# A two-layer hybrid decoder step in fp32: retention heads first, the gate chain spread over three quads, residual updates chunk by chunk

## What is computed

```python
h = rmsnorm(x, norm_mix_pre)
# one projection w_in, its columns shared out among 4 mLSTM, 4 retention and 8 gated-DeltaNet heads
proj = h @ w_in
y = concat(mlstm(...), retention(...), gated_delta(...)) @ w_out
x = x + rmsnorm(y, norm_mix_post)
h = rmsnorm(x, norm_mlp_pre)
x = x + rmsnorm(square(relu(h @ w_up)) @ w_down, norm_mlp_post)
```

## Time and profile before

| | us |
|---|---|
| median of 3 runs | 3286.99 (3285.19 to 3288.15) |
| the profiled execution | 3280.49 |
| its span | 3278.9 |
| TensorE busy in it | 3122.5 (95%) |
| DVE busy | 1930.1 (59%) |
| ACT busy | 1535.4 (47%) |

### The profile page before, as it was taken

The page is one execution under the profiler, slowest core; times in us unless marked ns, Lnnn a source line. Parts: engine busy times, 40 slices in busy tenths (PEclk is TensorE's granted clock), DMA queues, the critical chain, the costliest instruction groups (busy, mean ns, idle before and its releaser), DMA issues.

```text
span 3278.9 us, 72394 instructions
## 1 busy us (share of the span) xinstructions
PE 3122.5 (95%) x23264; PEld 3057.9 (93%) x23264; DVE 1930.1 (59%) x3923; ACT 1535.4 (47%) x3564; POOL 84.5 (3%) x161
## 2 busy tenths in 40 slices
PE   5999999998999999999869999999989999999997
PEld 5989999998999999999869989999989999999997
DVE  5677755656545545455567777556665455454555
ACT  4566654544433334334446666545444333343333
POOL 0000000000000000000010000000000000000000
PEclk9999999999999999999989999999999999999999
DMA  3344455643544444544423444555435444444454
GB/s 132 128 133 135 132 162 161 185 155 110 175 166 159 164 164 166 166 160 164 151 84 121 131 132 137 168 167 177 155 118 167 165 164 167 162 163 164 163 167 147
DMA packets 266061, 499.24 MB, mean 152 GB/s; under 512 B 34272, under 2 KB 39552, under 8 KB 265664
## 3 DMA queue, kind: packets, MB, share of 16 engines
q1 hardware_dynamic: 243360, 443.56, 41.3%
q0 software_dynamic: 14496, 51.05, 4.7%
q10 hardware_dynamic: 8064, 2.80, 0.3%
HBM read 475.30 MB, written 22.01 MB: 152 GB/s over the span
## 4 chain that ended last, share of the span: by engine, by line
PE 79%; DVE 9%; ACT 5%; issue 4%; DMA 2%; DVEq 1%; ACTq 0%; SPq 0%; POOLq 0%; POOL 0%
PE PU L455 71%; PE PABCD L455 4%; PE PE_ L455 2%; ACT Y L787 2%; PE PF L455 2%; ACT AE L787 1%; DVE WL L1156 1%; DMA RAW<-in_w 1%; ACT WH L787 1%; DVE Y L1170 1%; PE PABCD L458 1%; DVE Y L1321 1%; DVE AE L1500 1%; DVE X L1173 0%; PE PE_ L458 0%
## 5 line engine op out<-in xcount | busy, mean ns | idle before, releaser
L455 PE MATMUL PU<-HH,WH 128*128 128x288 f32 x4096 | 1285.4, 314 | 59.3 <-DVE HL L1161 48.0
L787 ACT ACTIVATE WH<-RAW 128x512 fp32r<-128x512 f32 x1669 | 965.2, 621 | 591.9 <-PE PU L455 437.5
L455 PE MATMUL PU<-HL,WH 128*128 128x288 f32 x4096 | 1212.6, 296 | 0.0
L455 PE MATMUL PU<-HH,WL 128*128 128x288 f32 x4096 | 1208.7, 295 | 0.0
L1156 DVE TENSOR_TENSOR WL<-RAW,WH 128x512 fp32r<-128x512 f32 x1668 | 1074.5, 687 | 223.0 <-ACT WH L787 205.8
L455 PEld LDWEIGHTS PU<-HH,WH 128*128 128x128 f32 x4096 | 774.6, 189 | 79.2 <-DVE HL L1161 49.4
L455 PEld LDWEIGHTS PU<-HL,WH 128*128 128x128 f32 x4096 | 775.8, 189 | 7.0
L455 PEld LDWEIGHTS PU<-HH,WL 128*128 128x128 f32 x4096 | 775.0, 189 | 0.0
L455 PE MATMUL PU<-UH,WH 128*128 128x288 f32 x2560 | 759.0, 296 | 3.2 <-DVE UL L1310 2.0
L455 PE MATMUL PU<-UL,WH 128*128 128x288 f32 x2560 | 755.2, 295 | 0.0
L455 PE MATMUL PU<-UH,WL 128*128 128x288 f32 x2560 | 752.7, 294 | 0.0
(11 more groups left out here) (245 smaller groups left out, 2244.4 us busy)
## 6 DMA issues: line engine op xcount, KB each, us to landing
RAW<-in_w SPq DMA_DIRECT2D x1669, 256.0 KB, 3.7
SIN<-in_sin POOLq DMA_DIRECT2D x32, 512.0 KB, 4.2
out_sout<-Y POOLq DMA_DIRECT2D x32, 512.0 KB, 5.3
BC<-gate_rows POOLq DMA_DIRECT2D x32, 304.0 KB, 4.3
AUX<-in_aux POOLq DMA_DIRECT2D x32, 152.0 KB, 3.4
X<-in_x SPq DMA_DIRECT2D x4, 576.0 KB, 7.5
out_y<-X SPq DMA_DIRECT2D x4, 576.0 KB, 2.8
Y<-in_gw POOLq DMA_DIRECT2D x2, 1024.0 KB, 5.0
```

Of the source, the lines that this page charges most:

```text
L455: return nc.tensor.matmul(out, lhsT, rhs, start=start, stop=stop, skip_group_check=True)
L787: return nc.scalar.activation(out, in_, f, **kw)
```

## The change

- **Order of heads.** After "first" come the four retention heads, then gated-DeltaNet (its first front stands in the last retention quad), then mLSTM. SP loads the units in that order from the same array; POOL's and ACT's stores go to the same places; `turn_of` gives the order of chunks in the output projection.
- **Gate projection.** GWf becomes two halves GW[0] (in SIN) and GW[1] (in Z1), loaded by `load_gate_weights` at the program's start, and for layer 1 behind the last head of layer 0; DVE multiplies them between the first splits of layer 0, and for layer 1 in the first `down_last` quad. TensorE makes the 16 matmuls in slots 0 to 7 of "first", two a slot, beside the norm's sums.
- **Gate chain.** Steps up to "decay" in "first" (slots 8 to 21), copies and scans in retention quad 0 (DVE: slots 1, 2, 3, 16, 28; ACT: 18, 20, 22), transposes and columns in retention quad 1 (slots 0, 2, 8). Several scratch tiles get other rooms. POOL's `store_rows` stands before the third retention head.
- **Chunk by chunk.** `update_and_split` follows each update of a pair with the HL of the pair before, and with a weight split after pairs 2, 4 and 6, both in `after_out` and at the turn to layer 1. ACT's `prenorm` makes HH and squares of each pair and the pieces 5 to 7 between. At the very start ACT and DVE go piece by piece through weights and x. The outer loop over layers is written out twice.

```diff
@@ walk
-            with eng.Fori(0, DEPTH) as l:
+            for l in range(DEPTH):
...
-                quad(q0, "first", l, None, (n0, l * H_C, 0, 0, p0))
+                quad(q0, "first", l, None)
+                for k in range(H_B - 1):
+                    quad(q0 + 1 + k, "ret", l, ret_head(k))
+                quad(q0 + H_B, "ret", l, ret_head(H_B - 1), gdn_head(0, 0, 0))
...
@@ POOL
+            def load_gate_weights(l):
+                if l:
+                    held("head_done", HEADS * l + 1)
+                    held("state_decayed", HEADS * l)
+                    held("state_read", HEADS * l)
+                for j in range(2):
+                    pool.dma_start(GW[j], d["gw"][l, :, j * (NC_ // 2):(j + 1) * (NC_ // 2)]).then_inc(sem("gate_weights_in"), 16)
...
             pool.dma_start(NG0[:], d["ng0"][0]).then_inc(sem("first_gain_in"), 16)
+            load_gate_weights(0)
             held("constants_in", 16 * len(con))
...
+                held(*gate("proj", l))
+                load_state(n0 + H_C)
+                for k in range(H_B):
+                    if k == 2:
+                        store_rows(l)
+                    head(n0 + k, n0 + H_C + k, n0 + H_C + k + 1 if k < H_B - 1 else n0, k % 2)
...
@@ TensorE
+            def gate_part(t, kind, l):
+                if kind == "first" and t < 8:
+                    if t == 0:
+                        pe.wait_ge(*gate("weights_a", l))
+                    if t == 4:
+                        pe.wait_ge(*gate("weights_b", l))
+                    if l == 0 and t % 2 == 0:
+                        pe.wait_ge(sem(f"x_in{t // 2}"), 16)
+                    pe.wait_ge(sem("x_updated"), 16 * l + t + 1)
+                    for k in (2 * t, 2 * t + 1):
+                        i = mm(PD[:, 0:T], GW[k // 8][:, k % 8], X[:, k], k == 0, k == NC_ - 1)
...
                 for t in range(SLOTS):
+                    if l:
+                        gate_part(t, kind, l)
+                    norm_part(t, kind, l, x)
                     unit_part(Q, t, kind, l, x, last_head is not None)
-                    norm_part(t, kind, l, x)
+                    if not l:
+                        gate_part(t, kind, l)
+                    if kind == "ret" and x[2] < 2:
+                        gates(t, x[2], l, x)
@@ ACT, prenorm
+                for g in range(NC_ // 2):
+                    if e == 0 and l == 0 and g % 2 == 0:
+                        hi_part(Q, g // 2)
+                        act.wait_ge(sem(f"x_in{g // 2}"), 16)
+                    act.wait_ge(sem("x_updated"), 16 * l + 4 * e + g + 1)
+                    for c in (2 * g, 2 * g + 1):
                         fn(HH[:, c], X[:, c], scale=gain[:, c:c + 1]).then_inc(sem("hh_ready"), 1)
+                    for c in (2 * g, 2 * g + 1):
+                        if c >= 4:
+                            act.wait_ge(sem("squares_summed"), NC_ * (2 * l + which) + c - 3)
                         fn(SQ[:, c % 4], X[:, c], ACT.Square).then_inc(sem("squares"), 1)
+                    if (e or l) and g in (1, 3, 5):
+                        hi_part(Q, g // 2 + 5)
+                if e == 0 and l == 0:
+                    for piece in range(4, 8):
+                        hi_part(Q, piece)
                 norm_scale("squares_summed", NC_ * (2 * l + e // 2 + 1), S, "s_ready")
...
@@ DVE
+            def update_and_split(l, which, gain, lo_l, lo_which, lo_gain, Q):
+                for g in range(8):
+                    update_x(l, which, gain, g)
+                    if g:
+                        prenorm_lo(lo_l, lo_which, lo_gain, range(2 * g - 2, 2 * g))
+                    if g in (2, 4, 6):
+                        lo_part(Q, g // 2 + 3)
+                prenorm_lo(lo_l, lo_which, lo_gain, range(14, 16))
+                lo_part(Q, 7)
+
+            def split_first(l):
+                if l:
+                    return
+                for c in range(4):
+                    lo_part(0, c)
+                    prenorm_lo(0, 0, NG0, range(4 * c, 4 * c + 4))
+                    if c < 2:
+                        gate_weights(0, c)
+                for piece in range(4, 8):
+                    lo_part(0, piece)
...
             def after_mlp(l):
-                for g in range(8):
-                    update_x(l, 1, NG[:, 2], g)
+                if l < DEPTH - 1:
+                    update_and_split(l, 1, NG[:, 2], l + 1, 0, NG0, (l + 1) * QUADS)
```

More of the change, by code:

```diff
@@ L260, in gdn_pair @@
                         h = 2 * i + par
-                        after = None if last and par else (n0 + h + 1, l * H_C + h + 1, h + 1, 1 - par, p0 + i + par)
-                        quad(q0 + 1 + h, "gdn", l, (n0 + h, l * H_C + h, h, par, p0 + i), after)
+                        after = None if last and par else gdn_head(h + 1, 1 - par, i + par)
+                        quad(q0 + 1 + H_B + h, "gdn", l, gdn_head(h, par, i), after)
                 with eng.Fori(0, H_C // 2 - 1) as i:
@@ L266, in walk @@
                 gdn_pair(H_C // 2 - 1, True)
-                with eng.Fori(0, H_B // 2) as i:
-                    for par in range(2):
-                        h = 2 * i + par
-                        quad(q0 + 1 + H_C + h, "ret", l, (n0 + H_C + h, l * H_B + h, h, par, p0 + H_C // 2 + i))
                 for h in range(H_A - 1):
@@ L341, in _, with next_units @@
                 sp.dma_start(X[:, k], d["x"][:, k]).then_inc(sem(f"x_in{c}"), 16)
-                load(c, 0)
+                load(c, 4 * H_C)
             for n in con:
                 sp.dma_start(con[n][:], d[n]).then_inc(sem("constants_in"), 16)
-            with sp.Fori(0, DEPTH * QUADS) as Q:
+            def next_units(Q, unit, after):
                 for s in range(4):
@@ L349, in _ @@
                         sp.wait_ge(sem("lo_ready"), 16 * Q + 4 * s + c + 1)
-                        load(c, 4 * Q + s + 1)
+                        load(c, unit + s + 1 if s < 3 else after)
+            for l in range(DEPTH):
+                q0, u0 = l * QUADS, l * (4 * QUADS)
+                with sp.Fori(0, H_B - 1) as k:
+                    next_units(q0 + k, u0 + 4 * H_C + 4 * k, u0 + 4 * H_C + 4 * k + 4)
+                next_units(q0 + H_B - 1, u0 + 4 * (H_C + H_B - 1), u0)
+                with sp.Fori(0, H_C - 1) as h:
+                    next_units(q0 + H_B + h, u0 + 4 * h, u0 + 4 * h + 4)
+                next_units(q0 + H_B + H_C - 1, u0 + 4 * (H_C - 1), u0 + 4 * (H_C + H_B))
+                with sp.Fori(H_C + H_B, QUADS - 1) as q:
+                    next_units(q0 + q, u0 + 4 * q, u0 + 4 * q + 4)
+                q = QUADS - 1
+                next_units(q0 + q, u0 + 4 * q, u0 + 4 * (QUADS + H_C) if l < DEPTH - 1 else 4 * DEPTH * QUADS)
             sp.wait_ge(sem("lo_ready"), 16 * DEPTH * QUADS + 1)
@@ L437, in _ @@
[L437 to L446 removed]
+                load_parameters(n0 + H_C, 0)
@@ L447, in _ @@
+                for h in range(H_C - 2, H_C):
+                    head(n0 + H_B + h, n0 + h, n0 + h + 1 if h < H_C - 1 else n0 + H_C + H_B, h % 2)
+                for h in range(H_C + H_B, HEADS):
+                    head(n0 + h, n0 + h, n0 + h + 1 if h < HEADS - 1 else None, h % 2)
+                if l < DEPTH - 1:
+                    load_gate_weights(l + 1)
             pool.wait_ge(sem("first_gain_in"), 16 * (DEPTH + 1))
@@ L1093, in mixer @@
                         if t == slot:
-                            linear_head(step, kind, x, last)
-                elif kind == "first":
-                    gates(t, l)
+                            linear_head(step, kind, l, x, last)
+                if kind in ("first", "ret"):
+                    gates(t, -1 if kind == "first" else x[2], l)
             def quad(Q, kind, l, x, front=None, last_head=None):
@@ L1112, in quad @@
                     joined = l if last_head else None
-                    if t % 2 and not (last_head and t == 13):
+                    if t % 2 and not (last_head and t == 13) and not (kind in ("first", "up_first") and t < 7):
                         if last_head and t == 15:
@@ L1605, in quad @@
                         evac(Q, 0, kind, l, x)
-                    if t % 2:
+                    if t % 2 and not (kind in ("first", "up_first") and t < 8):
                         lo_part(Q, t // 2 + 4, l if last_head else None)
@@ L1640, in _ @@
             dve.sem_inc(sem("x_updated"), 8)
-            for p in range(4):
-                lo_part(0, p)
-            walk(dve, lambda l: prenorm_lo(l, 0, NG0), quad, after_out, after_mlp)
+            walk(dve, split_first, quad, after_out, after_mlp)
 def kernel(**inputs):
```

249 lines of the change are left out of this document (121 added, 128 removed).

## The result

| | before | after |
|---|---|---|
| median (lowest to highest), us | 3286.09 (3284.32 to 3288.15) | 3252.45 (3250.14 to 3253.23) |
| the profiled execution, us | 3280.49 | 3252.05 |
| its span, us | 3278.9 | 3250.5 |

The ratio is 0.9896, with a 95% interval of 0.9879 to 0.9913. The gain is 33.6 us by the medians and 28.4 us between the two profiled executions. The forecast was 62.6, and the measured time lies above the range of 3210 to 3244.

What follows compares the result with a forecast made beforehand. TensorE, busy 95% of the span, was the bound. Start 31.3, turn to layer 1 35.3, MLP turns 3.4, restarts 4, minus 11.4 in retention quads: 62.6 us less, median 3224 (3216 to 3232; with neighbouring rivals 3210 to 3244).

Runs made afterwards that it cites:

- e1_pads: The changed kernel with 20 idle instructions at ACT's start and 40 at DVE's, nothing else moved: 3222.29 us, 0.9818 of before.

## What to carry to other kernels

Before a change that adds, removes or moves code ahead of a device loop, look for "issue" time right behind the loop's branch in the traces, and count the body's instructions on each engine. For bodies of 262 to 312 instructions, as here, where they happen to lie decided whether a jump back cost nothing or several us, and a few idle instructions ahead of the loop are the cheapest test. An idle piece that the profile puts down to nothing is a mechanism not yet known, and a sum that removes it should ask where else it can appear. Splitting a step into pieces between others pays only where another engine sets the pace of that stretch, so cost it for each place by itself.

## What was new of the hardware

- A jump back stopped ACT for 4.96 and then 2.37 us, in the next pass 5.28 and 1.61, and DVE for 2.75 and 3.17, or not at all, by the place of the loop's body in that engine's program. A shift by 20 instructions took ACT's away and one by 256 brought them back.
- A pair of stops of ACT, which is busy 47% of the time, made its quad 7.4 and 6.8 us longer than in e1_pads: TensorE waited in two places and was granted 0.93 and 0.97 of its clock in these quads.
- The same quad without the device's loop is 0.5 to 0.9 us of 44.5 shorter, with an equal busy time of TensorE.
- 512 KB took 8.5 and 10.5 us to land at the start of the program, where in the kernel before 1024 KB, issued at 22.0 us behind the loads of the start, had taken 5.0.
